# Moving the operand buffers of x, and everything behind them, by 64 bytes in each partition

## The reference, cut to what matters

```python
# first block
proj = h @ w_in[l]                       # 1024 -> all inputs of three branches
x = x + g1 * (merged @ w_out[l])
x = x + g2 * (jnp.square(jax.nn.relu(h2 @ mlp_w1[l])) @ mlp_w2[l])
# second block, twice
x = x + 0.5 * swiglu(rms_norm_2(x, ffn1_norm[l]), ffn1_w_gate[l], ffn1_w_up[l], ffn1_w_down[l])
proj = h @ w_in[l] + b_in[l]
y_attn = forgetting_attention(q, k, v, log_f) @ w_o_attn[l]
y_rnn = yr @ w_o_rnn[l]
x = x + merged @ w_out[l]
x = x + 0.5 * swiglu(rms_norm_2(x, ffn2_norm[l]), ffn2_w_gate[l], ffn2_w_up[l], ffn2_w_down[l])
```

## The kernel before

| tensor | first byte in the partition before | modulo 128 | modulo 128 after the change |
|---|---|---|---|
| w_hi, slot 0 | 13,440 | 0 | 0 |
| w_lo, slot 0 | 25,728 | 0 | 0 |
| a_hi (a_lo, b_hi, b_lo behind it, 16,384 bytes each) | 38,016 | 0 | 64 |
| xres | 103,552 | 0 | 64 |
| arena | 138,912 | 32 | 96 |
| q11_hi, then t_hi, q11_lo, t_lo | 147,104 | 32 | 96 |
| q_h and k_h of even pairs of heads | 175,808 | 64 | 0 |
| q_h and k_h of odd pairs of heads | 163,488 | 32 | 96 |

## Time and profile before

### The profile page before, as it was taken

The page is one execution under the profiler, slowest core; times in us unless marked ns, Lnnn a source line. Parts: engine busy times, 40 slices in busy tenths (PEclk is TensorE's granted clock), DMA queues, the critical chain, the costliest instruction groups (busy, mean ns, idle before and its releaser), DMA issues.

```text
span 3326.2 us, 52762 instructions
## 1 busy us (share of the span) xinstructions
PE 3306.1 (99%) x17742; PEld 2799.9 (84%) x17742; DVE 2169.9 (65%) x3377; ACT 1466.6 (44%) x2025; POOL 2127.7 (64%) x2188
## 2 busy tenths in 40 slices
PE   9999999999999999999999999999999999999999
PEld 5888777888889997788888899889987888888998
DVE  8887685544478878714435877788878334248886
ACT  4365664222243335735634333433347545533333
POOL 6444445555568886653356888698876544468886
PEclk9999999999999999999999999999999999999999
DMA  6221553322232323332223323232223222223232
GB/s 224 88 70 64 168 181 108 104 95 96 97 112 94 107 82 102 102 127 70 70 84 110 108 101 114 76 114 101 101 89 109 95 102 70 83 92 111 102 109 99
DMA packets 94485, 343.36 MB, mean 103 GB/s; under 512 B 10609, under 2 KB 11249, under 8 KB 93954
## 3 DMA queue, kind: packets, MB, share of 16 engines
q1 hardware_dynamic: 86978, 312.11, 27.4%
q10 hardware_dynamic: 7360, 29.29, 2.7%
HBM read 335.03 MB, written 2.13 MB: 101 GB/s over the span
## 4 chain that ended last, share of the span: by engine, by line
PE 52%; POOL 23%; issue 18%; DVE 2%; ACT 2%; DVEq 1%; POOLq 0%; ACTq 0%; DMA 0%
POOL w_lo L588 22%; PE ps L634 15%; PE ps L636 15%; PE ps L635 15%; POOL t_lo L588 1%; PE ps L1217 1%; PE ps L1199 1%; PE ps L801 1%; PE ps L802 1%; PE ps L803 1%; DVE arena L2771 1%; PE ps L1208 0%; DVEq L2773 0%; ACT w_hi L1305 0%; DVE arena L2172 0%
## 5 line engine op out<-in xcount | busy, mean ns | idle before, releaser
L588 POOL TENSOR_TENSOR w_lo<-raw,w_hi 128x256 fp32r<-128x256 f32 (+1 forms) x1680 | 1467.9, 904 | 1051.9 <-ACT w_hi L1305 1049.8
L634 PE MATMUL ps<-a_hi,w_lo 128*128 128x512 f32 (+1 forms) x2720 | 1019.3, 375 | 0.8 <-DVE a_lo L2118 0.3
L636 PE MATMUL ps<-a_hi,w_hi 128*128 128x512 f32 (+1 forms) x2720 | 1005.6, 370 | 0.0
L635 PE MATMUL ps<-a_lo,w_hi 128*128 128x512 f32 (+1 forms) x2720 | 1005.3, 370 | 0.0
L588 POOL TENSOR_TENSOR w_lo<-arena,w_hi 128x512 fp32r<-128x512 f32 x384 | 586.0, 1551 | 124.7 <-ACT w_hi L1785 121.3
L634 PEld LDWEIGHTS ps<-a_hi,w_lo 128*128 128x128 f32 x2720 | 512.6, 188 | 101.0 <-issue 18.3
L1305 ACT ACTIVATE w_hi<-raw 128x1024 fp32r<-128x1024 f32 x374 | 392.6, 1053 | 442.5 <-PE ps L636 424.0
L636 PEld LDWEIGHTS ps<-a_hi,w_hi 128*128 128x128 f32 x2720 | 512.6, 188 | 88.1
L635 PEld LDWEIGHTS ps<-a_lo,w_hi 128*128 128x128 f32 x2720 | 513.0, 189 | 81.2 <-issue 0.5
L634 PE MATMUL ps<-b_hi,w_lo 128*128 128x512 f32 x1088 | 425.9, 391 | 4.8 <-DVE b_lo L2190 4.0
L635 PE MATMUL ps<-b_lo,w_hi 128*128 128x512 f32 x1088 | 424.0, 390 | 0.0
(11 more groups left out here) (332 smaller groups left out, 4706.3 us busy)
## 6 DMA issues: line engine op xcount, KB each, us to landing
raw<-in_stream SPq DMA_DIRECT2D x471, 512.0 KB, 3.3
arena<-in_stream SPq DMA_DIRECT2D x96, 512.0 KB, 3.3
arena<-in_mod_w ACTq DMA_DIRECT2D x32, 512.0 KB, 4.2
arena<-in_mod_w SPq DMA_DIRECT2D x16, 512.0 KB, 11.6
arena<-arena ACTq DMA_DIRECT2D x16, 256.0 KB, 3.7
arena<-cum_rows ACTq DMA_DIRECT2D x2, 2048.0 KB, 9.2
xres<-in_x_t SPq DMA_DIRECT2D x4, 512.0 KB, 5.4
arena<-in_first SPq DMA_DIRECT2D x8, 256.0 KB, 11.8
```

The lines of the kernel that those rows point to most:

```text
L588: last = pool.tensor_tensor(to[:, at], of[:, at], hi[:, at].bitcast(F32), ALU.subtract)
L634: pe.matmul(out, lo, x_hi, start=start, stop=False)
L635: pe.matmul(out, hi, x_lo, start=False, stop=False)
L636: return pe.matmul(out, hi, x_hi, start=False, stop=stop)
```

## The change

One tensor of 16 numbers, 64 bytes in each partition, that nothing reads or writes is declared between `w_lo` and `a_hi`. `raw`, `w_hi` and `w_lo` stay where they are. Everything declared behind them begins 64 bytes further. No instruction is added or removed, and no size changes.

```diff
         w_hi = sb("w_hi", [P, RING, D], F32R)
         w_lo = sb("w_lo", [P, RING, D], F32R)
 
+        sb("shift_operands", [P, 16])
         a_hi, a_lo = sb("a_hi", [P, KT, S], F32R), sb("a_lo", [P, KT, S], F32R)
         b_hi, b_lo = sb("b_hi", [P, KT, S], F32R), sb("b_lo", [P, KT, S], F32R)
```

## The result

The kernel after took 3348.52 us (median of 4 runs, 3347.39 to 3356.27), the kernel before 3328.78 us beside it (4 runs). The ratio is 1.0065, with an interval of 1.0053 to 1.0076. The prediction was "no change, 3328.5 us, range 3318 to 3340", so the time lies outside the range and on the slower side.

A forecast was written before the change was run, and what follows sets the result against it. The prediction took PE's matmul pace to bound the kernel. All terms summed to 0: 3327.95 us for the profiled execution, plus 0.60 us to the median, about 3328.5 us, range 3318 to 3340.

The forecast's parts named there:

- What bounds the kernel: PE busy 3306.1 of 3326.2 us; only its matmul pace counts, 1 ns per matmul of x being worth 11.4 us.
- Stationary operands: Weight loads in all matmuls: a 64-byte move keeps each load in its class, judged from even-pair attention scores; cost 0.
- 11,424 x 2 ns = 23 us: Upper bound on the weight-load cost if even-pair scores hid up to 2 ns in the rounding; not taken.
- Moving operands: x in a, b, t and q: start matters in a step taken as 64 bytes, so 0; bounds -25 or -38 to +80 us.
- the faster rival: Matmuls of x in a and b: the moving operand's step exceeds 64 bytes, 25 to 38 us gained, 3290 to 3303 us; chance 0.12.
- The slower one: Matmuls of x in a and b: a start inside a longer line costs 7 ns each, 80 us, 3408 us; chance 0.08.
- Only t and q change class: Fast chunks' 256-column matmuls: t and q fall back to 120.0 ns, 8.4 us slower, 3337 us; chance 0.03.
- Other engines and transfers: ScalarE, DVE, POOL and loads into raw and arena: a 64-byte move costs 0, engines bounded at 1 us either way.

The follow-up runs named there:

- the benches: Two kernels computing nothing of the reference, TensorE alone running streams of 48 split matmuls at chosen places of x and weights; 512 columns took 226.7 ns at distance 0.
- the run with x alone: Against the kernel before, only a, b and xres moved by 64 bytes, params and arena kept at their old remainder modulo 128: 3336.06 us, ratio 1.0021.
- The run with everything moved: Against the kernel before, a 64-byte tensor declared ahead of raw, so weights and x both begin 64 bytes further: 3328.95 us, ratio 1.0000.
- those at 32, 96 and 128 bytes: Against the kernel after, the added tensor made 32, 96 or 128 bytes in place of 64: 3371.61, 3380.88 and 3368.03 us.
- the second bench: TensorE alone, other cases: x moved up to 1,088 bytes, weights moved, one weight column repeated; 512 columns 226.9, 228.9, 232.5, 233.3 ns at 0, 64, 128, 192.
- the first bench: TensorE alone, 144 cases: x at 0 to 240 bytes, weights at 0, 32 and 64 past a multiple of 128; 226.7 to 236.7 ns by place.

## Why the prediction was wrong

**What bounds the kernel: right.** PE is busy 99% in both, every term of the loss is PE's pace, and its waits stayed but for the one of the profiled execution. The count of matmuls and the worth of a nanosecond (11.4 us) held.

**Stationary operands: the step that failed.** "In that place a weight load at remainder 64 runs beside a moving operand at remainder 0, so the two are 64 bytes apart, as they are everywhere after the change ... Cost: 0." The row itself was read rightly. In the unrounded starts of the trace the score follows a_hi after 226 or 227 ns in all 20 such places of even pairs, and after 232 to 234 ns in all 26 of odd pairs, which is the 7 ns of the prediction. What failed is carrying it over, in two ways. The direction: there the load lay 64 bytes ahead of x (by the table, q_h at 175,808 and a_hi at 38,016, x minus load = 192 modulo 256), and after the change x lies 64 bytes ahead of the load. The kind of load: it was a plain float32 load in front of a score, and not the float32r stream that fills the time. In the benches that stream takes 233.3 ns at 192 and 228.9 at 64, so at the very distance of the even pairs it is 6.6 ns slower than what the row shows. A cost of 0 for one says nothing of the other. In the stream a single interval would not do either: at 64 it takes 229, 232 and 226 ns in turn, and one of the three is as short as that of before. The prediction even had a bound from this row, "11,424 x 2 ns = 23 us", and put it aside. That it came near the truth is luck, since it was the rounding of another kind of event: by the run with x alone, 6,624 x 1.73 ns for a and 3,264 x 2.03 ns for b make 18.1 us.

**Moving operands: wrong in kind.** The prediction looked for a step in each operand's own remainder and chose 64 bytes for it. The run with everything moved shows that the remainder of x doesn't matter by itself, and those at 32, 96 and 128 bytes that 512-column x has no free class among these but 0. That t is quicker at 32 than a at 0 was read rightly, but it is no rule for x: at a distance of 32 a 256-column matmul gains 2.2 to 3.4 ns in the bench and a 512-column one loses 6.7 ns. The gain that the faster rival took from it, 2.2 to 3.3 ns on 11,424 matmuls, came true only for the 1,536 halves of a, -3.0 us, and for the values, -4.4 us, which it didn't count.

**The rivals.** The slower one had the right sign and the wrong size: 80 us at 7 ns a matmul, measured 20 us in all. At 32 and 96 bytes 512-column x loses 5.8 to 6.4 ns in the kernel, so its price was good for a distance that the change didn't have. "Only t and q change class" was a true part, 8.1 us in the changed kernel and 7.8 us by itself, against 8.4 predicted; it had been taken as an alternative to x's slowing and not as an addition.

**Other engines and transfers: right.** ScalarE's conversions took 1060 and 1062 ns in place of 1061 and 1063, loads 3.3 us. The scores' longest record is 593 ns against 595.

**The range.** Its upper end, 3340, took in t and q but not the 23 us bound of the row on which the zero rested. With 23 us in it the range would have reached 3352 and held the time.

**What stays open.** Why the pace depends on these distances in these amounts, and which part of the memory or of TensorE's reading makes it so. Why some streams have two stable paces: at a distance of 192 and the same addresses the second bench gave 113.3 or 117.8 ns by what ran ahead of them, the kernel gave 117.5 to 117.8 at 64 and 113.3 at 192 in most products, and 512-column x in the kernel after took 228.9 and 233.3 ns. And why the load of a float32 score at a distance of 192 costs nothing where a float32r stream pays 6.6 ns.

## What to carry to other kernels

When TensorE is the bound, a tensor declared anywhere between the weights and x is an edit of the matmuls: look at the distance between the moving operand and the stationary one modulo 256 bytes, keep it at 0 for 512 columns of float32r, and try 192 for 256 columns. A cost of 1% per instruction is read from dozens of starts in a row, of the same kind of matmul and in the same direction as in the place that the change touches. Where the trace has only another kind of event, it doesn't bound the stream, and the range has to hold the price of the rival. A pace gained in a dense stretch is only worth what the engine that prepares the weights lets through.

## What the runs showed of the hardware

- Matmuls of 512 columns of float32r follow one another in 226.7 ns at best, and only with x and weights at a distance of 0 modulo 256 bytes (or, in the first bench, at 112 with the weights at 32 or 64 bytes); 228.9 at 64 (and 233.3 in 9% of those steps of the kernel after), 232 to 234 elsewhere at multiples of 32. Moving both operands together by 64 bytes changes nothing in the kernel.
- Matmuls of 256 columns have another order: 120.0 ns at 0 and 96, 118.7 or 120.0 at 128, 116.6 or 117.8 at 32, and 113.3 at 112, and at 64 and 192 where they fall into the quicker of two cycles.
- The dependence goes when the weight load reads one column over and over (231.7 ns at 0, 32, 64 and 96, 231.1 at 128), but that load is not quicker than a good distance.
- A whole kernel that is otherwise the same gets 1.3% slower with 32 bytes between weights and x and 1.6% slower with 96.
- A plain float32 load 64 bytes ahead of the moving float32r operand (even pairs) left the interval at 226 or 227 ns, one 32 bytes ahead (odd pairs) made it 232 to 234 ns.
